# Twelve layers of two transformers on one core: attention run pair by pair of heads behind the projections

## What is computed

```python
def rms_norm(x, g):
    return x * rsqrt(mean(x * x, axis=-1) + EPS) * g

# stick: 16 heads of 64; z = q k / 8, weights of key s: exp(z - sum over later keys of softplus(z))
# dsa: q, k normed per head and rotated; index heads score the keys, the 64 best per query stay
def dsa(h):
    score = einsum('bqh,bqhs->bqs', wi, relu(einsum('bqhd,bsd->bqhs', qi, ki)))
    keep = top_k(score, 64)
    p = softmax(where(keep, q @ k.T * 64 ** -0.5, -inf))
    return (p @ v) @ w_out

# multi: 16 heads, q and k normed per head; 6 + 6 of them rotated, 4 of them with a bias table
def multi(x):
    o = softmax(q @ k.T * 64 ** -0.5 + bias) @ v
    o = concat(rms_norm(o[na]), rms_norm(o[dilated]), rms_norm(o[gq]))
    return x + o @ w_out
```

## Time and profile before

| what | value |
|---|---|
| median of 3 runs | 2528.54 us (2527.0 to 2528.85) |
| profiled execution | 2532.53 us, its span 2530.8 |
| busy: TensorE matmul, VectorE, ScalarE, POOL | 93%, 62%, 47%, 7% |
| DMA | 327 MB, weights' queue 38.4% of 16 engines |
| TensorE's granted clock in 40 slices, in tenths | 8889999999999999998899988899999999999999 |
| chain that ended last | TensorE 80%, VectorE 11%, ScalarE 5%, issue 2% |

### The profile page before, as it was taken

One profiled execution on the slowest core, in us unless ns is written; L12 is line 12 of the kernel. 1 busy time (PEld: TensorE's weight loads), 2 busy tenths in 40 slices (PEclk: granted clock), 3 DMA queues, 4 the chain that ended last, 5 costly groups with the idle time before them and its releaser, 6 DMA issues.

```text
span 2530.8 us, 55813 instructions
## 1 busy us (share of the span) xinstructions
PE 2361.4 (93%) x22886; PEld 2207.9 (87%) x22886; DVE 1579.6 (62%) x2350; ACT 1192.0 (47%) x1988; POOL 174.2 (7%) x249
## 2 busy tenths in 40 slices
PE   6799899998999998999987998999999999998999
PEld 5689799998899997599976897999986999977998
DVE  6744365665665666666577543655666777766776
ACT  5533444435544462654455333544556444556443
POOL 1000010010100111010010000100210000211000
PEclk8889999999999998899988899999999999999999
DMA  4220155542455341165522201555422554423553
GB/s 170 92 85 4 44 189 193 177 139 75 136 188 197 129 154 63 42 202 180 191 75 92 84 4 44 183 196 177 142 92 80 190 179 166 150 67 110 187 177 125
DMA packets 88434, 327.16 MB, mean 129 GB/s; under 512 B 9808, under 2 KB 9936, under 8 KB 87632
## 3 DMA queue, kind: packets, MB, share of 16 engines
q1 hardware_dynamic: 87984, 322.72, 38.4%
q0 software_dynamic: 288, 2.10, 0.2%
HBM read 323.73 MB, written 1.05 MB: 128 GB/s over the span
## 4 chain that ended last, share of the span: by engine, by line
PE 80%; DVE 11%; ACT 5%; issue 2%; POOL 1%; DMA 0%; DVEq 0%; ACTq 0%; SPq 0%; POOLq 0%
PE bank L1220 16%; PE bank L1221 16%; PE bank L1222 16%; PE bank L1242 4%; PE bank L1243 4%; PE bank L1244 4%; DVE w_split L1784 3%; ACT w_split L1514 2%; PE bank L491 2%; PE bank L1410 2%; PE bank L500 1%; DVE h_split L1812 1%; PE bank L1389 1%; PE bank L514 1%; PE bank L1400 1%
## 5 line engine op out<-in xcount | busy, mean ns | idle before, releaser
L1220 PE MATMUL bank<-h_split,w_split 128*128 128x256 f32 x3168 | 920.6, 291 | 36.4 <-DVE h_split L1812 22.8
L1221 PE MATMUL bank<-h_split,w_split 128*128 128x256 f32 x3168 | 905.3, 286 | 0.0
L1222 PE MATMUL bank<-h_split,w_split 128*128 128x256 f32 x3168 | 904.1, 285 | 0.0
L1784 DVE TENSOR_TENSOR w_split<-ring_a,w_split 128x1024 fp32r<-128x1024 f32 x468 | 569.1, 1242 | 208.6 <-ACT w_split L1514 207.2
L1220 PEld LDWEIGHTS bank<-h_split,w_split 128*128 128x128 f32 x3168 | 611.5, 193 | 52.9 <-DVE h_split L1812 32.5
L1221 PEld LDWEIGHTS bank<-h_split,w_split 128*128 128x128 f32 x3168 | 606.6, 191 | 2.1
L1222 PEld LDWEIGHTS bank<-h_split,w_split 128*128 128x128 f32 x3168 | 606.1, 191 | 0.0
L1514 ACT ACTIVATE w_split<-ring_a 128x1024 fp32r<-128x1024 f32 x468 | 476.8, 1049 | 133.8 <-PE bank L1222 122.1
L1242 PE MATMUL bank<-act_split,d_split 128*128 128x256 f32 x1008 | 285.1, 283 | 2.4 <-DVE act_last L1861 2.4
L1243 PE MATMUL bank<-act_split,d_split 128*128 128x256 f32 x1008 | 285.1, 283 | 0.0
L1244 PE MATMUL bank<-act_split,d_split 128*128 128x256 f32 x1008 | 285.0, 283 | 0.0
(11 more groups left out here) (277 smaller groups left out, 3300.5 us busy)
## 6 DMA issues: line engine op xcount, KB each, us to landing
ring_a<-wa SPq DMA_DIRECT2D x474, 512.0 KB, 4.4
ring_d<-wd SPq DMA_DIRECT2D x132, 512.0 KB, 4.4
tab_sb<-tab SPq DMA_DIRECT2D x1, 2448.0 KB, 13.3
planes<-na POOLq DMA_DIRECT2D x2, 1024.0 KB, 6.5
xT<-x SPq DMA_DIRECT2D x1, 1024.0 KB, 4.8
out<-xT SPq DMA_DIRECT2D x1, 1024.0 KB, 3.9
vec_sb<-vec SPq DMA_DIRECT2D x1, 288.0 KB, 4.9
tab_sb<-tab SPq DMA_DIRECT2D x1, 65.0 KB, 4.6
```

The source lines that it names most:

```text
L1220: mm(dst, w[:, 0, ks], x[:, 0, k, :], start=(k == 0), stop=False)
L1221: mm(dst, w[:, 0, ks], x[:, 1, k, :], start=False, stop=False)
L1222: last = mm(dst, w[:, 1, ks], x[:, 0, k, :], start=False, stop=(k == KT - 1))
L1784: v.tensor_tensor(w_split[:, u % 4, 1, :], ring_a[:, u % 4, :], w_split[:, u % 4, 0, :].bitcast(f32), ALU.subtract).then_inc(s["w_lo"], 1)
```

## The change

The attention layers get one program for each engine, `att_pe`, `att_act`, `att_dve`, `att_pool`, written over **slots**: slot n is unit n with what each engine does around it. Weights are laid out so that units 3t, 3t+1, 3t+2 are q, k and v of the pair of heads t (`in_pairs`; in dsa after six index units, `FIRST`). `pair_at(L, n, b)` gives the pair whose first unit lies b slots back, once in three slots, and each engine runs that pair's steps there; in dsa the softmax steps come six slots later (`LAG`). Further:

- scores, value products and z of two heads are issued alternately on the two halves of the array, without a padded copy of k; POOL's clears and copies go;
- V is turned pair by pair, and ScalarE copies it back over `qkv`;
- dsa's selection takes two rounds of eight in each of slots 12 to 15;
- the output projection goes by contraction tiles: unit k takes one pair's outputs and adds to all eight output tiles, which lie in four banks until the end; then four additions of 128 x 512 (`add_banks`);
- the unit banks are three instead of four; the pairs of a multi layer are reordered (`PAIR_ORDER`, the neighbourhood heads last), its norm segments are (0,3), (3,6), (6,8);
- the squares of the norm ahead of FFN and attention layers are made by ScalarE (`squares`), TensorE sums them in eight matmuls, behind unit 1.

```diff
+FIRST = {"stick": 0, "dsa": 6, "multi": 0}
+LAG = {"stick": 0, "dsa": 6, "multi": 0}
+GAIN_OF = {"stick": 0, "dsa": 0, "multi": 1}
+OUT_SLOTS = {"stick": (0, 1, 2, 3, 4, 5, 6, 7), "dsa": (0, 1, 2, 3, 4, 7, 10, 12), "multi": (0, 1, 2, 3, 4, 5, 6, 7)}
+PAIR_ORDER = (2, 3, 4, 5, 6, 7, 0, 1)
...
+            def scores(t):
+
+                pe.wait_ge(s["qk_ready"], tiles + 2 * t + 2)
...
+                for qt in range(NT):
+                    for e in range(2):
+                        h = slice(HD * e, HD * e + HD)
+                        last = mm(B[e][:, qt * S:(qt + 1) * S], qkv[h, t, qt * P:(qt + 1) * P], qkv[h, 8 + t, :],
+                                  start=True, stop=True)
+                last.then_inc(s["s_done"], 2)
...
+            def out_unit(k):
+
+                pe.wait_ge(s["w_lo"], L["us"] + N + k + 1)
+                pe.wait_ge(s["o_ready"], 8 * L["mixers"] + k + 1)
+                w, x = w_split[:, (u + N + k) % 4, :, :], x_split[2]
+                for m in range(KT):
+                    if k == 0 and m % 2 == 0:
+                        bank_free(OUT_BANKS[kind][m // 2])
+                    o, ms = B[OUT_BANKS[kind][m // 2]][:, (m % 2) * S:(m % 2 + 1) * S], slice(m * P, (m + 1) * P)
+                    mm(o, w[:, 0, ms], x[:, 0, k, :], start=(k == 0 and m % 2 == 0), stop=False, skip_group_check=True)
+                    mm(o, w[:, 0, ms], x[:, 1, k, :], start=False, stop=False, skip_group_check=True)
+                    last = mm(o, w[:, 1, ms], x[:, 0, k, :], start=False, stop=(k == KT - 1), skip_group_check=True)
+                    if k == KT - 1 and m in (1, 3, 5):
+                        last.then_inc(s["out_done"], 1)
+                last.then_inc(s["a_used"], 1)
...
+            for n in range(N + OUT_SLOTS[kind][-1] + 1):
+                if n < N:
+                    one(n)
+                elif n - N in OUT_SLOTS[kind]:
+                    out_unit(OUT_SLOTS[kind].index(n - N))
...
+                t = pair_at(L, n, 8 + lag)
+                if t is not None:
+                    pv(t)
+                t = pair_at(L, n, 7 + lag)
+                if t is not None:
+                    turn(t, 1)
+                t = pair_at(L, n, 6 + lag)
+                if t is not None:
+                    turn(t, 0)
+                if kind == "multi" and n in (16, 24):
+                    segment_sum(n // 8 - 2)
+                t = pair_at(L, n, 4 + lag)
+                if t is not None:
+                    scores(t)
+                t = pair_at(L, n, 3)
+                if t is not None:
+                    turn_v(t)
+                t = pair_at(L, n, 2)
+                if t is not None:
+                    norm_rope(2 * t + 1)
+                t = pair_at(L, n, 1)
+                if t is not None:
+                    norm_rope(2 * t)
+                if kind == "multi" and n == pv_slot(L, 7):
+                    segment_sum(2)
...
+                t = pair_at(L, n, 7 + lag)
+                if t is not None:
+                    copy_turned(t, 0)
+                t = pair_at(L, n, 8 + lag)
+                if t is not None:
+                    copy_turned(t, 1)
+                t = pair_at(L, n, 9 + lag)
+                if t is not None:
+                    out_pair(t)
+                if kind == "multi" and n in (17, 25):
...
+                t = pair_at(L, n, 5 + lag)
+                if t is not None:
+                    exps(t)
...
+                    index_rope(n - 2)
+                t = pair_at(L, n, 3)
+                if t is not None:
+                    norm_rope(2 * t + 1)
+                t = pair_at(L, n, 2)
+                if t is not None:
+                    norm_rope(2 * t)
+                t = pair_at(L, n, 5 + lag)
+                if t is not None:
+                    shifted(t)
+                if 0 < n < N + KT - AHEAD:
+                    lo(L, n + AHEAD)
+                t = pair_at(L, n, 6 + lag)
+                if t is not None:
+                    normed(2 * t)
+                    normed(2 * t + 1)
...
-                        last = mm(norm_bank(m)[:, 0:S], T("ones"), sq[:, k, :], start=(k == 0), stop=(k == 1))
+                    for k in range(KT):
+                        pe.wait_ge(s["squared"], 4 * L["hs"] + k // 2 + 1)
+                        last = mm(norm_bank(m)[:, 0:S], T("ones"), sq[:, k, :], start=(k == 0), stop=(k == KT - 1))
                 last.then_inc(s["ssum_ready"], 1)
...
+            def squares(b):
+
+                x2, q2 = [t[:, 2 * b:2 * b + 2, :].rearrange("p a b -> p (a b)") for t in (xT, sq)]
+                A(q2, x2, ACT.Square).then_inc(s["squared"], 1)
...
-            def sum_squares(L):
-
-                for b in range(4):
-                    pool.wait_ge(s["x_added"], 8 * L["part"] + 2 * b + 2)
-                    x2, q2 = [t[:, 2 * b:2 * b + 2, :].rearrange("p a b -> p (a b)") for t in (xT, sq)]
-                    pstep.did(nc.gpsimd.tensor_tensor(q2, x2, x2, ALU.mult))
...
-SEGMENTS = [(0, 2), (2, 5), (5, 8)]
+SEGMENTS = [(0, 3), (3, 6), (6, 8)]
...
```

More of the change, by code:

```diff
@@ L118, in plan_layers @@
                         convs=sum(o["kind"] == "ffn" and o["idx"] >= 4 for o in out),
+                        outs=sum(o["kind"] not in ("ffn", "rwkv") for o in out),
                         multis=sum(o["kind"] == "multi" for o in out)))
@@ L1139, in rwkv_pool, with unit_bank, norm_rope_bank, squared @@
                 g_.tensor_scalar(sq[:, k, 0:1], hT[:, k, 0:1], -1.0, None, ALU.mult).then_inc(s["xx_ready"], 1)
+        OUT_BANKS = {"multi": (4, 2, 5, 7), "dsa": (4, 2, 5, 7), "stick": (4, 7, 0, 5)}
+        def unit_bank(s):
+            return B[4 + s % 3]
+        def norm_rope_bank(L, n):
+            return B[(7, 2)[(n + (L["kind"] == "dsa")) % 2 == 0]]
+        def squared(i):
+            return extra[:, i % 4, :]
+        def gained_(i):
+            return extra[:, 4 + i % 4, :]
+        def root_(i):
+            return work[:, i % 4, :]
@@ new lines, in att_pool, with times_cos @@
+        def att_pool(pool, L):
+            def times_cos(n):
+                i = n - (5 if L["kind"] == "dsa" else 0)
+                rope = rope_of(L["kind"], i // 2) if i >= 0 else "0"
+                if rope:
+                    x = gained_(i) if i >= 0 else qkv[:, 24 + n, :]
+                    pool.wait_ge(s["nr_mm"], L["tiles"] + n + 1)
+                    nc.gpsimd.tensor_tensor(x, x, T("cos" + rope), ALU.mult).then_inc(s["cos_ready"], 1)
+            if L["kind"] == "multi":
+                pool.wait_ge(s["h_ready"], 8 * (L["hs"] + 1))
+                pool.dma_start(hT[:, :, :].rearrange("p a b -> p (a b)"), na_in[L["idx"], :, :])\
+                    .then_inc(s["na_loaded"], 16)
+            for n in range(21 if L["kind"] == "dsa" else 16):
+                times_cos(n)
@@ L1497, in _ @@
                     pe.wait_ge(s["tab_loaded"], 16)
-                dict(ffn=ffn, stick=stick, dsa=dsa, multi=multi,
-                     rwkv=lambda L: rwkv_pe(pe, L, product, out_proj))[L["kind"]](L)
+                if L["kind"] == "ffn":
+                    ffn(L)
+                elif L["kind"] == "rwkv":
+                    rwkv_pe(pe, L, product, out_proj)
+                else:
+                    att_pe(pe, L, unit, norm)
         @block.scalar
@@ L1544, in norm @@
                 else:
+                    if not after_mixer:
+                        for b in range(4):
+                            squares(b)
                     root_table()
@@ L1765, in _ @@
                     act.wait_ge(s["tab_loaded"], 16)
-                dict(ffn=ffn, stick=stick, dsa=dsa, multi=multi,
-                     rwkv=lambda L: rwkv_act(act, L, A, hi, root_table, inverse_root))[L["kind"]](L)
+                if L["kind"] == "ffn":
+                    ffn(L)
+                elif L["kind"] == "rwkv":
+                    rwkv_act(act, L, A, hi, root_table, inverse_root)
+                else:
+                    att_act(act, L, A, hi, root, step, inverse_root)
         @block.vector
@@ L2102, in _ @@
                     dve.wait_ge(s["tab_loaded"], 16)
-                dict(ffn=ffn, stick=stick, dsa=dsa, multi=multi,
-                     rwkv=lambda L: rwkv_dve(dve, L, v, step, lo, add_out))[L["kind"]](L)
+                if L["kind"] == "ffn":
+                    ffn(L)
+                elif L["kind"] == "rwkv":
+                    rwkv_dve(dve, L, v, step, lo, add_out)
+                else:
+                    att_dve(dve, L, v, step, lo, rms_inverse, add_banks)
         @block.gpsimd
@@ L2264, in blocks, with in_pairs @@
     return w.reshape(KT, P, n, P).transpose(2, 1, 0, 3).reshape(n, P, KT * P)
+def in_pairs(b, order=range(KT)):
+    return np.stack([b[[t, KT + t, 2 * KT + t]] for t in order]).reshape(3 * KT, P, D)
 def padded(w, n):
```

1127 lines of the change are left out of this document (525 added, 602 removed).

## The result

The change makes the kernel slower: 2581.6 us (2577.8 to 2583.4, 4 runs) against 2528.7, ratio 1.0208, 95% interval 1.019 to 1.0225. The forecast was 2555 us with a range of 2495 to 2590. The profiled execution took 2580.0 us with a span of 2578.2, 1.6 under its median, where that of before was 3.8 above: the spans differ by 47.4 us, the medians by 53.

The account below looks back on a forecast made before the run. The prediction took a ring of waits through the engines' queues, with TensorE idling and its clock falling, as the bound: layers and squares -24.7, clock +52, together +27 on 2528.5, so 2555 us, range 2495 to 2590.

Parts of the forecast that it names:

- The ring: Roped passes in multi and dsa: waits through VectorE, ScalarE and TensorE take 17.8 us (dsa 18.1), TensorE idling 4.0.
- TensorE's own work: A roped pass of three slots: units, norm steps, turns, scores and values need 13.8 us of TensorE.
- Rival C: Multi and dsa passes: no ring, passes run at 13.8 us, no clock falls, 2430 us; chance 0.11.
- Rival D: Multi and dsa passes: longer ring, POOL's cosine slowing VectorE, 2 us more in each of 19, about 2595; chance 0.10.
- The clock: New TensorE idles of 3.4 us and more in multi and dsa: 27 x 5/6 x 2.3 = +52 us.
- 5 of 6: Share of long TensorE idles outside the starts, in the kernel before, after which the clock fell; applied to 27 new idles.
- Rival B: Multi and dsa passes: the ring holds but the clock stays at 2.4 GHz in most, 2504 us; chance 0.19.
- the 62: Clock term in multi and dsa by the skill's rule, all 27 idles answered: 62 us instead of 52.
- The layers at full clock: Layer sums without clock loss: dsa 215.2 us (+0.4), each multi layer 175.6 (+6.7 for both).
- Stick: Stick attention layer: no ring, 127.2 us against 149.8, -22.6, with 3.74 of head work for each of eight pairs.
- 1.7 for each of four steps from attention to FFN: FFN starts behind attention: gain of 1.7 us each from squares leaving POOL and the later norm, within a -9.2 term.
- The other half of this term: Layers behind an FFN: squares off POOL and later norm bring unit 1's end from +13.8 to +10.9 us.

Follow-up runs that it names:

- e2: The change with seven added useless matmuls (3.0 us) ahead of each turn of a pair's first head, where TensorE idles: 2553.3 us.
- e7: The change with ScalarE's copy of a pair's output one slot earlier and VectorE's slot beginning with the scaling of both heads: 2498.2 us.
- e9: e8 with ScalarE copying the first head's turned probabilities ahead of squaring the even tile instead of behind it: 2457.3 us.
- e1: The change with ScalarE's root of a pair's odd tile moved ahead of the earlier pair's exponentials, in the same slot: 2580.3 us.
- e4: The change with squares and their sum back on POOL and two norm matmuls instead of eight, still behind unit 1: 2608.8 us.
- e8: e7 with the eight norm matmuls behind unit 0 of a layer instead of unit 1, in FFN and attention layers: 2489.3 us.
- e5: The change with VectorE's scaling of the first head's probabilities ahead of the weight's low half instead of behind it: 2535.5 us.
- e6: e2 with three added matmuls (1.3 us) instead of seven: 2558.8 us.
- e3: e1 with VectorE's scaling of the first head's probabilities ahead of the weight's low half as well: 2524.1 us.

## Why the prediction was right, and where it was off

**The ring.** Right. 17.8 us were given (the terms as listed add to 17.9), 17.9 measured with the clock held (e2), in dsa 18.1 against 18.2, an idle of 4.0 against 3.77. e7 and e9 show that only the order of its steps makes it: the same steps in another order have no such wait. Incomplete: between exponentials and scaling the root is one of two ways (e1).

**TensorE's own work.** 13.8 worked out, 13.9 measured in e9. Rival C's pass length exists, but in another kernel than the one shown. Rival D is not seen: beside POOL's cosine the low half in the ring took its usual 1.22 us (rows under e4).

**The clock.** Right in kind, and near in size. It fell behind every new idle of 3 us and more, not 5 of 6. The share by which the clock stays below 1.00 in the windows is already half of the slowed time: 239.9 x 0.12 = 28.8, 192.6 x 0.11 = 21.2, 191.1 x 0.10 = 19.1, in all 69 us. That is too much for a loss, since a slowed stretch often begins inside the idle, where a slow clock costs nothing (the stretch at 1891.00 above). Half of the time in which TensorE was busy at half clock is 24.8, 18.0 and 16.4, about 59 us, where the term said 52: 25 slowed stretches of 2.4 us each where 22.5 of 2.3 were put in. In a pass of the first multi layer e2 gives 2.6 us, where this count gives 2.9 and half of the whole stretch 3.4. Rival B is refuted: the clock falls. The Trainium skill, "TensorE: Matmul & The Clock Gate", section "HAM oscillation — how this bites in real kernels", has every such pass slowed anew; the trace agrees in each of them, and the 62 that the prediction worked out by it is nearer than its 52.

Two readings behind this term were weak. The kernel before has more long idles than the six that were counted: 3.31 to 4.80 us in the rwkv layers (95.82, 110.32, 122.14, 301.03, 1375.38, 1390.55, 1568.32) and 2.48 us ahead of both multi output projections (1933.50, 2302.41). The clock was at half behind all of them, so five of six was too low a share. And before is not at full clock either: the same count gives it 32 us in these three layers, so of the 64 us by which dsa and the two multi layers grew, some 28 are the clock and some 36 would be there at full clock too.

**The layers at full clock.** Taking those losses off, dsa is 215.1 (forecast 215.2), the multi layers 174.6 and 174.7 (175.6 each). The sums agree within 2 us in all; whether each part of them does was not looked at singly. Stick is 130.6 instead of 127.2, at a clock of 1.00 and with TensorE busy for 129.0. A pass there takes 12.65 us where 3 x 2.88 + 3.74 = 12.38 were put in, which is 2.2 of the 3.4 over eight pairs; the rest lies at the ends of the layer. The value product of one pair and of the next:

```profile
568.74 0.65 PE L1349 MATMUL bank<-planes,qkv 128*64 128x256 f32 x4
581.39 0.65 PE L1349 MATMUL bank<-planes,qkv 128*64 128x256 f32 x4
```

**The step that failed** is "1.7 for each of four steps from attention to FFN". The FFN layers behind attention take 195.1, 197.8, 198.1 and 198.1 us from the last output matmul to their own last one, against 197.0, 194.2, 195.7 and 195.7 before: together 6.5 slower, where 6.8 faster were put in. The stretch from the last output matmul to the first down projection, before, behind multi and behind stick, and after in the same two places:

```profile
1960.90:1976.80 15.90, 13.52 (x103) 12.60 (x102) 11.87 (x16) 10.27 (x14) 3.83 (x4) 1.00 0.56 192
672.60:691.30 18.70, 16.32 (x103) 15.14 (x102) 12.30 (x15) 11.35 (x15) 3.82 (x4) 0.82 0.51 174
```

```profile
1985.60:2003.80 18.20, 16.02 (x115) 14.92 (x114) 10.34 (x18) 12.33 (x20) 0.00 (x0) 1.00 0.28 88
650.40:667.00 16.60, 15.89 (x115) 14.90 (x113) 8.88 (x15) 12.22 (x20) 0.00 (x0) 1.00 0.36 117
```

I had read the 18.7 us behind stick, in which the clock was 0.82, and taken it for all four; the others are 15.9. After, the eight norm matmuls take 3.6 us and stand behind unit 1, so the root and the first down projection come later; what POOL no longer costs was hidden there before, behind output units that still ran. e8 takes back 1.7 of it behind multi. The other half of this term held: ahead of stick, unit 1 and the norm end at 10.8 us behind the FFN, forecast 10.9.

The sum: of 47.4 us by which the span grew, the forecast had 27.3. The steps to the FFN add 13.3, the clock 7.2, stick 3.4; dsa and multi at full clock take back 2.0, the rwkv layers and the FFNs behind them 1.8. So the largest miss is not in the ring or the clock, and 2581.6 lies inside the forecast's own range of 2533 to 2585, close to its upper end. The other parts of the change (three unit banks instead of four, the output projection by contraction tiles, the new order of pairs) were not run apart; that they cost nothing by themselves is not shown.

## What to carry to other kernels

Steps of one iteration hidden behind other work cost nothing only if no chain of waits through several engines' queues is longer than the bottleneck engine's own work in a pass; add up that chain with the order in which each queue is written, side ways included, before counting busy shares. When a loop's idle is of a size that the clock answered elsewhere in the trace (count all such idles, not a few), price it at idle plus half of the slowed time in which the engine works. To break such a chain, move what the waiting engine needs next to the head of each queue; cutting one of two parallel ways gives nothing (e1), cutting their common end does (e5).

## What the runs showed of the hardware

Idles of 2.5 us ahead of a turn were answered by the clock in some passes and not in others of the same kernel, with the same idle to 0.01 us (e6, above; in e5 one of four in the first multi layer and three of three in dsa; the longest that was not answered is 2.74 us, in e5 at 952.55). Idles of 3.0 us and more were answered each time, in every kernel (that ahead of the first matmul aside). Idles of 0.93 to 1.62 us, once or twice a pass, were not answered in the passes of e3 (multi), e7 and e8, and of four of 1.7 us one was; but in dsa's passes of e3 two, with a short stretch between them, were, in three passes of three. TensorE there, and the window behind it:

```profile
965.41 0.66 PE L1253 MATMUL bank<-tab_sb,planes 128*128 128x128 f32 x4 [0.93 <-DVE planes L1666]
965.90 0.38 PE L1224 MATMUL bank<-tab_sb,qkv 128*128 128x128 f32 x2
968.17 0.36 PE L1876 MATMUL bank<-h_split,w_split 128*128 128x256 f32 x1 [1.90 <-issue]
```

```profile
968.90:972.50 3.60, 3.60 (x20) 3.60 (x19) 1.22 (x1) 2.05 (x4) 0.00 (x0) 0.53 0.22 83
```

What decides at these sizes stays open; it was not tried apart from the kernels above.
